# First modulation in eight chunks of channels, and a new order of mLSTM steps, passage and last tiles, in a hybrid attention, mLSTM and convolution layer

## The reference

```python
mod = (silu(cond) @ w_ada + b_ada).reshape(-1, 6, D)          # shift1, scale1, gate1, shift2, scale2, gate2
h = rmsnorm(x, g_pre_mix) * (1 + scale1) + shift1
(na_q, na_k, na_v, m_q, m_k, m_v, m_o, m_i, m_f,
 cv_b, cv_c, cv_x, gate_pre) = split(h @ w_in)
att = attention(na_q, na_k, na_v)                 # context: full; latent: 2-D neighbourhood + cached context
hm = bidir_mlstm(m_q, m_k, m_v, m_i, m_f)         # 4 heads, chunks of 128 tokens, forwards and backwards
hm = headwise_norm(hm) * m_norm_g * sigmoid(m_o)
hc = cv_b * short_conv(cv_c * cv_x, conv_w)
g = sigmoid(gate_pre + b_gate)                    # three gates per channel
merged = g[0] * (att @ w_br_na) + g[1] * (hm @ w_br_m) + g[2] * (hc @ w_br_cv)
x = x + gate1 * rmsnorm(merged @ w_out, g_post_mix)
h2 = rmsnorm(x, g_pre_ffn) * (1 + scale2) + shift2
x = x + gate2 * rmsnorm((silu(h2 @ w_ffn_gate) * (h2 @ w_ffn_up)) @ w_ffn_down, g_post_ffn)
```

## Time and profile before

| | us |
|---|---|
| median of 3 runs | 1171.06 (1169.77 to 1174.03) |
| the profiled execution's own time | 1170.69 |
| its span in the profile | 1167.8 |
| mean granted TensorE clock | 0.995 |
| PE busy | 1138.1 |
| DVE busy | 717.9 |
| ACT busy | 472.0 |
| POOL busy | 67.9 |

### The profile page before, as it was taken

How to read it: one execution, slowest core, us unless ns; L and a number is a source line. 1 busy time by engine, 2 the same in 40 slices (tenths; PEclk the granted TensorE clock), 3 DMA queues, 4 the chain that set the end, 5 groups by cost and what they waited for, 6 DMA issues and landing times. The chain is left out here.

```text
span 1167.8 us, 18659 instructions
## 1 busy us (share of the span) xinstructions
PE 1138.1 (97%) x7438; PEld 1070.8 (92%) x7438; DVE 717.9 (61%) x1277; ACT 472.0 (40%) x864; POOL 67.9 (6%) x119
## 2 busy tenths in 40 slices
PE   5999999999999999999999999899999999999997
PEld 4799999889999999999999987899999999988886
DVE  4434545439565555488785455799997777633444
ACT  4334344443323333322322336565555555633431
POOL 1032110000000000040000002100000000000002
PEclk8999999999999999999999999999999999999999
DMA  9456221122432111245554144233422223315112
GB/s 364 185 190 127 72 73 56 37 90 79 70 60 65 55 55 58 88 126 178 183 196 147 55 162 145 90 109 127 145 91 88 94 109 106 113 54 188 64 36 90
DMA packets 40006, 129.17 MB, mean 111 GB/s; under 512 B 8720, under 2 KB 10288, under 8 KB 38512
## 3 DMA queue, kind: packets, MB, share of 16 engines
q1 hardware_dynamic: 36592, 121.41, 32.4%
q0 software_dynamic: 3328, 6.57, 2.1%
HBM read 120.59 MB, written 7.36 MB: 110 GB/s over the span
## 5 line engine op out<-in xcount | busy, mean ns | idle before, releaser
L1996 PE MATMUL ps<-h_hi,w_lo 128*128 128x320 f32 x1184 | 366.5, 310 | 0.0
L1994 PE MATMUL ps<-h_hi,w_hi 128*128 128x320 f32 x1024 | 323.1, 315 | 0.2 <-DVE w_hi L1547 0.2
L1995 PE MATMUL ps<-h_lo,w_hi 128*128 128x320 f32 x1024 | 317.0, 310 | 0.0
L1996 PEld LDWEIGHTS ps<-h_hi,w_lo 128*128 128x128 f32 x1184 | 222.9, 188 | 0.0
L1421 DVE TENSOR_TENSOR w_lo<-raw,w_hi 128x1024 fp32r<-128x1024 f32 x109 | 132.4, 1225 | 119.1 <-ACT w_hi L1067 118.1
L1994 PEld LDWEIGHTS ps<-h_hi,w_hi 128*128 128x128 f32 x1024 | 193.0, 188 | 2.3 <-DVE w_hi L1547 0.5
L1995 PEld LDWEIGHTS ps<-h_lo,w_hi 128*128 128x128 f32 x1024 | 193.0, 189 | 0.0
L1994 PE MATMUL ps<-w_hi,h_hi 128*128 128x512 f32 x380 | 151.2, 398 | 3.4 <-DVE h_lo L1697 3.4
L1995 PE MATMUL ps<-w_lo,h_hi 128*128 128x512 f32 x380 | 148.9, 392 | 0.0
L1996 PE MATMUL ps<-w_hi,h_lo 128*128 128x512 f32 x380 | 148.8, 392 | 0.0
L1067 ACT ACTIVATE w_hi<-raw 128x1024 fp32r<-128x1024 f32 x109 | 113.1, 1052 | 35.1 <-PE ps L1996 34.7
(11 more groups left out here) (267 smaller groups left out, 1834.7 us busy)
## 6 DMA issues: line engine op xcount, KB each, us to landing
raw<-in_w_blocks SPq DMA_DIRECT2D x182, 512.0 KB, 3.6
ada<-in_w_first SPq DMA_DIRECT2D x8, 1024.0 KB, 18.0
xline<-x SPq DMA_DIRECT2D x5, 512.0 KB, 5.0
x<-xline SPq DMA_DIRECT2D x5, 512.0 KB, 7.8
xt<-in_x_sample SPq DMA_DIRECT2D x4, 512.0 KB, 6.8
vtok<-vline POOLq DMA_DIRECT2D x8, 256.0 KB, 9.8
g<-gline SPq DMA_DIRECT2D x2, 1024.0 KB, 6.4
xb<-in_x_sample SPq DMA_DIRECT2D x4, 512.0 KB, 4.3
```

The source lines that it names most:

```text
L1994: nc.tensor.matmul(dst, wh, xh, start=first, stop=False, skip_group_check=resumed)
L1995: nc.tensor.matmul(dst, wh, xl, start=False, stop=False, skip_group_check=resumed)
L1996: return nc.tensor.matmul(dst, wl, xh, start=False, stop=last, skip_group_check=resumed)
```

## The change

The eight units of the first modulation are laid out anew: unit k holds, for the 128 channels of chunk k, the columns of scale and of shift. So a chunk needs one unit, one group of rows and one of columns (4 matmuls where a pair had 8). The plan then goes chunk by chunk: rows and columns of chunk 0, the fifth turn of x, `h` of chunk 0, rows and columns of chunk 1; and from then on chunk k's products for the first two token tiles, rows of chunk k + 2, the products for the other three tiles, columns, `h` and `hsplit` of chunk k + 2. SP issues a block of weights behind every second unit, units 0, 2, 4 and 6. `mif` stands between chunks 6 and 7, `mifs` behind the value tiles.

Attention: the list of side steps begins with an empty entry, and in the last token tile of mv each of the four parts takes a side step. mLSTM: `mcols` stands ahead of the last tile of cx 0 instead of the first of cb 0, and the empty entry ahead of the steps is gone, so all half steps come one slot earlier. Passage: the splits of the feed-forward part's first blocks, `square2`, `resid`, `scale2` of the last two token tiles are in another order. Last tiles: each `final` stands ahead of the next tile's product instead of behind it. The diff, cut to these parts:

```diff
@@ -69,8 +69,8 @@
 
     u = []
     ada = lambda which, i: ("ada", (which, i), KD, UW)
-    for i in range(4):
-        u += [ada(1, i), ada(0, i)]
+    for k in range(KD):
+        u.append(ada("first", k))
     u.append(("v", 0, KD, 512))
     for p in range(2):
         u += [("q", p, KD, UW), ("k", p, KD, UW)]
...
@@ -234,7 +234,7 @@
                 plan.append(("mscan",))
             if UNITS[n][:2] == ("cx", 0) and j == 0:
                 plan.append(("mnat",))
-            if UNITS[n][:2] == ("cb", 0) and j == 0:
+            if UNITS[n][:2] == ("cx", 0) and j == 3:
                 plan.append(("mcols",))
             if side and (kind != "br" or j % 2 == 0 or UNITS[n][:2] == ("br", (2, 3))):
                 plan.extend(side.pop(0))
...
@@ -252,42 +252,45 @@
                 held.append(("conv", UNITS[n][1], x["what"][0]))
 
     for step, t in (("xsq", 0), ("xsq", 1), ("xturn", 0), ("xsq", 2), ("xsq", 3), ("xturn", 1), ("xsq", 4),
-                    ("xturn", 2), ("xturn", 3), ("xturn", 4)):
+                    ("xturn", 2), ("xturn", 3)):
         plan.append((step, t))
 
-    def first_rows(i):
-        group("ada_row", 2 * i, bank=4)
-        group("ada_row", 2 * i + 1, bank=5)
-
-    def first_cols(i):
-        group("ada_pair", 2 * i + 1, bank=6)
+    def rows(k):
+        group("ada_row", k, bank=4 + k % 2)
+
+    def columns(k):
+        group("ada_pair", k, bank=6)
 
     mif = UNIT_OF[("mif", 0)]
-    first_rows(0)
-    first_cols(0)
-    plan.append(("h", 0))
+    rows(0)
+    columns(0)
+    plan += [("xturn", 4), ("h", 0)]
     split_to(1)
-    plan += [("hsplit", 0), ("h", 1), ("hsplit", 1), ("first", 0)]
-    first_rows(1)
-    split_to(2)
-    first_cols(1)
-    plan += [("h", 2), ("h", 3), ("hsplit", 2), ("hsplit", 3), ("first", 1)]
-    for i in (2, 3):
-        first_rows(i)
-        split_to(i + 1)
-        plan.append(("first", 2 * i - 2))
-        first_cols(i)
-        plan += [("h", 2 * i), ("h", 2 * i + 1), ("hsplit", 2 * i), ("hsplit", 2 * i + 1), ("first", 2 * i - 1)]
-    group("mif", mif, 0, 0, bank=4)
-    group("mif", mif, 0, 1, bank=5)
-    split_to(6)
-    plan.append(("first", 6))
-    group("mifs", mif, 0, 0, bank=6)
-    group("mifs", mif, 0, 1, bank=4)
-    plan.append(("first", 7))
+    plan.append(("hsplit", 0))
+    rows(1)
+    columns(1)
+    plan += [("h", 1), ("hsplit", 1)]
+    for k in range(KD):
+        plan.append(("first", k, 0, 2))
+        if k + 2 < KD:
+            rows(k + 2)
+        plan.append(("first", k, 2, TT))
+        if k + 2 < KD:
+            columns(k + 2)
+            if k % 2 == 0:
+                split_to(k // 2 + 2)
+            plan += [("h", k + 2), ("hsplit", k + 2)]
+        if k == 5:
+            split_to(5)
+        if k == 6:
+            group("mif", mif, 0, 0, bank=4)
+            group("mif", mif, 0, 1, bank=5)
+            split_to(6)
     split_to(7)
     for t in range(TT):
         group("v", FIRST_ADA, t, bank=t if t < 4 else 7)
+    group("mifs", mif, 0, 0, bank=6)
+    group("mifs", mif, 0, 1, bank=4)
     plan.append(("kc",))
     plan.append(("bias0",))
     plan.append(("vout",))
...
@@ -307,7 +310,7 @@
                         if t == 0:
                             split_to(BLOCK_OF[n, 3] + 1)
                             plan.append(("use", BLOCK_OF[n, j]))
-                        if side and j % 2 == 0:
+                        if side and (j % 2 == 0 or t == TT - 1):
                             plan.extend(side.pop(0))
                         if j < 3:
                             plan.append(("part", "mv", 0, t, j))
...
@@ -324,10 +327,10 @@
         if kind == "k":
             if which == 0:
                 N = len(NA_UNITS)
+                side.append([])
                 for s in range(N + 2):
                     side += [[("na", 0, s)], [("na", 1, s)]]
         if kind == "cx" and which == 0:
-            side.append([])
             for s in range(len(ML_UNITS)):
                 side += [[("ml", 0, s)], [("ml", 1, s)]]
         if kind == "mo" and which == 0:
...
@@ -369,8 +372,6 @@
             if j == 3:
                 if t == TT - 1:
                     plan.append(("resid", 3))
-                    split_to(ff0 + 3)
-                    plan.append(("square2", 3))
                 group("out", m, 1, t, bank=(5, 6, 7, 4, 6)[t])
             else:
                 plan.append(("part", "out", 1, t, j))
...
@@ -381,13 +382,15 @@
     def ff_group(k, i, f, h):
         group(k, UNIT_OF[(k, i)], f, h, bank=(4 if k == "fu" else 0) + 2 * h + f)
 
-    plan += [("scale2", 3), ("resid", 4), ("square2", 4), ("use", ff0)]
-    plan.append(("scale2", 4))
+    split_to(ff0 + 2)
+    plan += [("square2", 3), ("resid", 4)]
+    split_to(ff0 + 3)
+    plan += [("scale2", 3), ("square2", 4), ("use", ff0)]
+    ff_group("fg", 0, 0, 0)
     split_to(ff0 + 4)
-    ff_group("fg", 0, 0, 0)
     plan.append(("use", ff0 + 1))
     ff_group("fg", 0, 1, 0)
-    plan += [("turn2", 3), ("split2", 3), ("use", ff0 + 2)]
+    plan += [("turn2", 3), ("scale2", 4), ("split2", 3), ("use", ff0 + 2)]
     ff_group("fu", 0, 0, 0)
     plan += [("turn2", 4), ("split2", 4), ("use", ff0 + 3)]
     ff_group("fu", 0, 1, 0)
...
@@ -432,11 +435,9 @@
             use(m, *range(parts_of(m)))
             for t in range(TT):
                 if i == 5:
-                    if c == 1 and t == TT - 1:
+                    if c == 1 and t:
                         plan.append(("final", t - 1))
                     group("down", m, c, t, bank=(5 * c + t) % 8)
-                    if c == 1 and 0 < t < TT - 1:
-                        plan.append(("final", t - 1))
                     if c == 1 and t == TT - 1:
                         plan.append(("final", t))
                 else:
...
@@ -830,10 +831,10 @@
                 sp.dma_start(xt[:, t, :], src).then_inc(x_in[t], 16)
                 if t == 0:
                     sp.dma_start(cst[:, 0:160], a["consts"][:, 0:160]).then_inc(const_in, 16)
-            for i in range(4):
-                for j in (2 * i, 2 * i + 1):
-                    sp.dma_start(ada0[:, j, :], a["w_first"][j]).then_inc(ada_in[j], 16)
-                load(i)
+            for j in range(KD):
+                sp.dma_start(ada0[:, j, :], a["w_first"][j]).then_inc(ada_in[j], 16)
+                if j % 2 == 0:
+                    load(j // 2)
             sp.dma_start(cst[:, 160:640], a["consts"][:, 160:640]).then_inc(const2_in, 16)
             sp.dma_start(wm[:, :, :], a["w_mif"]).then_inc(wm_in, 16)
             sp.dma_start(kct[:, :, :], a["cache_k"]).then_inc(kc_in, 16)
...
@@ -2042,14 +2042,12 @@
                                                    start=(o == 0), stop=(o == 1))
                 elif kind == "ada_pair":
                     pe.wait_ge(act_drain, drains("A", gid("ada_row", which)))
-                    if which == (0, 0):
+                    if which[1] == 0:
                         pe.wait_ge(xt_dve, 3)
                         pe.wait_ge(xt_act, 2)
                     for m in range(2):
-                        for k in range(2):
-                            o = 4 * m + 2 * k
-                            ins = nc.tensor.matmul(full[:, o:o + 2], adarow[:, m, k * P:(k + 1) * P], sel,
-                                                   start=True, stop=True)
+                        ins = nc.tensor.matmul(full[:, 2 * m:2 * m + 2], adarow[:, ada_slot(n), m * P:(m + 1) * P],
+                                               sel, start=True, stop=True)
                 elif kind == "mif":
                     f, h = what
                     pe.wait_ge(wm_in, 16)
...
@@ -2098,12 +2096,12 @@
                 if k % 2 == 0:
                     block_ready(BLOCK_OF[n, k // 2])
                 pe.wait_ge(h_lod, k + 1)
-                for t in range(TT):
+                for t in range(t0, t1):
                     ins = three(ps[:, t if t < 4 else 7, :], h_hi[:, k, tok(t)], h_lo[:, k, tok(t)],
                                 weight(w_hi, n, k), weight(w_lo, n, k), k == 0, k == KD - 1)
                     if k == KD - 1:
                         ins.then_inc(gemm_done, 1)
-                if k in (1, 3, 5):
+                if k in (1, 3, 5) and t1 == TT:
                     ins.then_inc(first_done, 1)
 
             def mv_part(t, j):
```

More of the change, by code:

```diff
@@ L869, in _ @@
                 elif step[0] == "kc":
-                    sp.wait_ge(gemm_done, gid("ada_row", (0, 3)) + 1)
+                    sp.wait_ge(gemm_done, gid("ada_row", ("first", KD - 1)) + 1)
                     load_bias(sp, br0_in, 0)
@@ L978, in _ @@
                     pool.wait_ge(gemm_done, gid("mifs", 0, 0, 1) + 1)
-                    pool.wait_ge(gemm_done, gid("ada_row", (0, 3)) + 1)
+                    pool.wait_ge(gemm_done, gid("ada_row", ("first", KD - 1)) + 1)
                     nc.gpsimd.memset(bm[:, :, :, 256:NKEY], 0.0).then_inc(bias_zero, 1)
@@ L1686, in _ @@
                     dve.wait_ge(xt_dve, TT)
```

(13 more changed lines are left out.)

15 lines of the change are left out of this document (7 added, 8 removed).

## The result

The changed kernel took 1160.97 us (median of 4 executions) beside 1170.61 for the kernel before: a ratio of 0.9912, 95% interval 0.9886 to 0.9938. Two more sets on other chips gave 1162.72 (0.9936, 0.9921 to 0.9952) and 1161.13 (0.9928, 0.9916 to 0.9941). The gain is 6.7 to 9.6 us by the medians. The 14 executions have a median of 1161.7 and a mean of 1161.5; each set against the mean of before beside it gives 10.3, 7.5 and 8.9, or 8.8 over all. The forecast was 6.2. The case "faster by over 0.5%" came true, and "within 0.5%" had been given a little more. The median of 1160.97 lies 0.03 under the range of 1161.0 to 1170.0, and the two repeats lie in it: which side of that end the time fell on is chance, that it fell so far from the 1165.0 is not.

What follows compares the result with a forecast made beforehand. TensorE bounds the kernel, busy 1138.1 of 1167.8 us, so gains are waits: start stage 1.3, attention 0.6, mLSTM 2.4, passage 1.3, last tiles 0.6, sum 6.2, giving 1164.5 profiled, 1165.0 median; range 1161.0 to 1170.0.

Steps and rivals of the forecast that it cites:

- faster by over 0.5%: Whole kernel: outcome below 1165.2 us, a gain of over 5.9 us; chance 0.43.
- within 0.5%: Whole kernel: outcome within 5.9 us of before; chance 0.50.
- "adarow" 0.6, fragments -1.3: First modulation: 0.6 us wait for the row copy goes; more, smaller row and column groups cost 1.3, bounds 0 and 1.8.
- clock at the start: First modulation: low clock near 24 us stays away (+2.4), ends sooner, or lasts longer (-1.1); taken as +0.7 us.
- mLSTM stalls: mLSTM steps: PE's waits for the weights of three steps, 3.9 us in all, go.
- early turns: mLSTM statistics' turns one tile earlier: new 1.0 us wait for "mnat", 0.5 at the first step; cost 1.5, bounds 1.0 and 3.0.
- passage: Passage into the feed-forward part: block and evacuation 2 us sooner, first wide product gains 1.3 us, bounds 0.3 and 1.8.
- A: mLSTM shift gives its gain back: steps 6 and 8 not ready, early turns cost 3.0; 1168.8 us, chance 0.20.
- C: Clock stays low through the chunked stage because of thin rows and columns; 1173 us with 20 us low, chance 0.07.
- D: Start doesn't move, the fifth turn's copy ending as late as before, and fragments cost 1.8; 1166.8 us, chance 0.08.
- B: Clock stays up at the start (+1.7 to the sum) and at the statistics' turns (+1.5); 1161.8 us, chance 0.15.
- E: Turns don't hold the clock: it falls before the first product, stays low 2 us longer; 1166.8 us, chance 0.04.

Runs made afterwards that it cites:

- turns spread among products: Changed kernel with each set of the statistics' turns emitted behind one chunk of the next tile's products: 1163.69 us (0.9947).
- turns in the old place with early steps: Changed kernel with "mcols" back right ahead of the first mLSTM step, which stays one tile earlier: 1163.79 us (0.9942).
- modulation alone: Kernel before with only the change's first modulation edits (rows, columns, loads, "first_unit"): 1168.04 us (0.9985).
- attention alone: Kernel before with only the attention steps begun one tile later and two of them one part apart at their end: 1168.59 us (0.9985).
- mLSTM alone: Kernel before with only the statistics' turns one tile earlier and no empty slot ahead of the steps: 1166.87 us (0.9979).
- passage alone: Kernel before with only the change's whole passage edit (hunks 6 and 7 of the diff): 1167.88 us (0.9982).
- last tiles alone: Kernel before with only the finals of the last tiles each ahead of the next drain (hunk 8): 1169.29 us (0.9991).
- filled pauses: Unused extra turns in TensorE's early pause: twelve in the changed kernel, 1159.34 us (0.991); twenty-two in the kernel before, 1166.23 us (0.9971).
- the moved scale: Kernel before with only the fifth row block's scale moved behind the evacuation of the passage's fourth turn: 1168.84 us (0.999).

## Why the prediction was right and wrong

The same clocks and landmarks over all profiles give each term its size. The start's low stretch: with the old start 6.8 us in six profiles and 3.4 in two; with the new one 6.8, four times 3.4, and none twice. At the turns of the statistics: in their old place 3.4 us in eight profiles, none in two; in the early place 3.4 in three, 6.8 in three. (Not counted are the turns spread among products, 3.4, and the turns in the old place with early steps, where PE waited 1.6 right behind them, 6.8.) At the fifth turn of the passage: 3.4 us in three of seven with the old passage, each worth 0.75; in none with the new one. One such place, from the profile of the modulation alone:

```profile
742.00:744.00 2.00, 2.00 (x11) 2.00 (x10) 2.00 (x5) 1.87 (x5) 0.00 (x0) 0.56 0.36 145
744.00:746.00 2.00, 2.00 (x10) 2.00 (x9) 1.30 (x4) 1.12 (x3) 0.00 (x0) 0.59 0.00 0
```

| term | predicted | measured | by |
|---|---|---|---|
| start | 1.3 | 1.5 | first product from the last scaling of x, 9 and 9 profiles |
| "adarow" 0.6, fragments -1.3 | -0.7 | -0.3 | 40.64 to 40.96 at clock 1.00 |
| clock at the start | 0.7 | 1.0 | mean loss 2.2 (42.84 to 40.64, 8 profiles) and 1.25 (42.21 to 40.96, 7) |
| attention | 0.6 | 0.8, less 0.25 | attention alone; modulation alone |
| mLSTM stalls | 3.9 | 4.4 | steps' starts, change and mLSTM alone |
| early turns | -1.5 | -0.9 | first step against the attention's output turn |
| clock at the turns | 0 | -1.1 | mean 5.1 us low against 2.7 |
| passage | 1.3 | 2.1, and 0.3 of clock | passage alone |
| last tiles | 0.6 | 0.6 | last tiles alone |
| sum | 6.2 | 8.1 | medians: 6.7 to 9.6 |

The sum is about spans, and there it fits: the 75 executions of before that ran beside the experiments have a mean span of 1167.85, the 14 of the change 1159.64, 8.2 less. The forecast also held "the span and 2.9 around it" fixed. What lies around the span is 2.2 us in the mean of those 75 (1.8 to 3.7) and 1.9 in the 14 (1.8 to 2.0), so another 0.4 came from there. Why is open.

**Right.** The mechanisms: the first product, the single wait for "mnat", the three stalls that go, the passage's wait, POOL's short step (0.27 for 0.84, beside a drain that reads PSUM, as the rule of the Trainium skill, "SBUF — State Buffer", section "SBUF: two separate sides", has it). Rivals A, C and D did not come. Of A there is the part that the early turns lengthen the low clock, 1.1 us on average, which the sum had at 0; the prediction had the size of such a fall (1.5) but not that the place decides how often it comes. B, the better clock, came in part: at the start, and only in some executions. Its 1161.8 is nearest to the time measured, but by luck: none of the change's three profiles has the clock up in both places, and most of the gain came from other terms.

**E, and the rule behind it.** Twelve turns in the pause hold the clock at 1.00, where nothing else is on PE. The prediction's own evidence, turns alone "at 14 to 16 us at 1.00", was misread. The profile's first record of the clock begins at 15.32 us in before, and the column shows 1.00 wherever there is no record. The turns themselves tell the level. The windows of before for L2168 alone (us, PE busy (x), clock, DMA, GB/s):

```profile
13.00:14.00 1.00, 1.00 (x6) 1.00 1.01 426
16.00:17.00 1.00, 1.00 (x11) 1.00 1.06 434
```

Up to 15.3 a turn's matmul starts every 0.21 us, from there on every 0.11: TensorE was at its low level and came up at 15.3, though the column reads 1.00 in both lines. So a tile's eight turns took 1.7 us and then 0.9, and the prediction's 1.1 was a mixture. All 18 profiles show the same step of pace at the clock's first record, and in 17 of them PE had run nothing but turns in the 4 us ahead of it. So turns alone bring the clock up as well as hold it. The Trainium skill, "TensorE: Matmul & The Clock Gate", Part 4, states of transposes that the full clock "doesn't engage" for them, since such work "doesn't count as PE-busy the same way"; no profile here agrees, and both the rise and the filled pauses speak directly against it.

**Wrong by size, four terms.** (1) The passage: the step that failed is "The fifth turn gains 1.6, the low halves 1.5, DVE's sums 1.3". The sum took 1.3 for this term, with 1.8 as its upper bound; it measured 2.1. The step let the gain shrink along the chain. DVE's evacuation of the fourth turn starts 5.51 behind that turn in before and 3.32 in after, 2.19 sooner; the list from there to the sum (evacuation, low half, drain, evacuation, low half, drain) takes 7.34 in before and 7.42 in after. It moved as one piece:

```profile
735.66 1.36 DVE L1955 TENSOR_SCALAR h<-ps,mod 128x128 f32<-128x128 f32 x4
737.80 1.30 DVE L1964 TENSOR_TENSOR h_lo<-h,h_hi 128x512 fp32r<-128x512 f32 x2 [0.78 <-ACT h_hi L1404]
739.01 0.49 DVE L1540 TENSOR_TENSOR ff<-ps,sg 128x320 f32<-128x320 f32 x1
739.41 1.36 DVE L1955 TENSOR_SCALAR h<-ps,mod 128x128 f32<-128x128 f32 x4
741.47 1.29 DVE L1964 TENSOR_TENSOR h_lo<-h,h_hi 128x512 fp32r<-128x512 f32 x2 [0.70 <-ACT h_hi L1404]
```

(2) The stalls: the three rows add to 3.9, and PE got 4.4 back, 0.1 to 0.2 for each on top of its row. (3) The early turns: the 1.0 was 0.8, and the 0.5 behind the next tile did not show, for that tile ran at the low clock and DVE's copies (done at 284.2) were hidden behind it. (4) The fragments: 0.9 instead of 1.3 (what is left of the net 0.3 when the 0.6 for "adarow" is taken as forecast), within the bounds of 0 and 1.8. A likely reason, not tested: the fixed cost of a group of 32 was charged in full to a group of 16. Of the 1.9 between 6.2 and 8.1, 0.8 is the passage with 0.3 more of its clock, 0.5 the stalls, 0.6 the early turns, 0.4 the fragments, 0.3 and 0.2 the clock and start, against 1.1 for the clock at the turns and 0.1 in the attention. The range was too narrow above all on the passage, whose upper bound of 1.8 lies under the 2.1 measured, then on the early turns (lower bound 1.0, measured 0.9), and on the clock: the 14 executions of one kernel spread over 4.4 us.

**The version that came out.** With the steps in their old places and only DVE's other work moved behind them, the kernel takes 1158.36 (0.9901, up to 0.9914), 3.4 us less than the change's median; the intervals of the change's second and third set begin above it (0.9921 and 0.9916), that of the first overlaps it. The landmarks account for 0.5 of the 3.4 (the 0.9 of the shift less the last wait of 0.4) and the clock for some 1.1 to 1.5; the rest is not explained.

## What to carry to other kernels

Where PE waits for a product of DVE's queue, look first at what stands in that queue ahead of it: moving two convolutions and one low half behind it won the stalls without the cost of moving the step and what it depends on. When the first member of a fixed chain moves, price the whole chain by that move. Each wait row that went here gave 0.1 to 0.2 us more than it said. Pauses and thin matmuls are priced by the clock behind them as well: fill a pause on the critical path's engine if a bank is free (worth 2.4 us by the medians in the change, and nothing more where the steps stood in their old places), and compare several profiles before giving a clock fall to an edit. Ahead of the clock's first record, read the level from the pace of the matmuls and not from the column.

## What the runs showed of the hardware

- Turns (f32 transposes of 128x128) alone bring TensorE's clock up: in 17 of 18 profiles PE ran nothing but turns in the 4 us before their pace went from one matmul per 0.21 us to one per 0.11, at 11.8 to 17.0 us.
- A pause of 1.8 to 3.4 us on PE after thin work was followed by 3.4 or 6.8 us at 0.50 in 13 of 15 profiles, and in none of three where turns filled it. The same kernel showed 6.8, 3.4 and none in three executions.
- A fall is not tied to a pause: 3.1 us of 36-row turns and 4-column matmuls without one were followed by one of 3.4 us in 8 of 10 profiles; with 0.8 of wait ahead of them it lasted 6.8 in half.
- Alternating 36-row f32 turns with the split products costs 0.3 us for each round trip (1.01 us for 0.25 and 0.44 of work).
- A wait of 0.4 to 0.5 us for the "vtok" transfer in the attention stands in 2 of 18 profiles (the mLSTM part alone, the moved scale), neither of which touches it: a landmark between two single profiles carries that much chance.
